# Levels 1 to 4 of a block inverse by 32x32 tiles, biases as a row of the low-rank products, and both square roots under one table

## The reference

```python
w_log = -jax.nn.softplus(-(w0 + jnp.tanh(xw @ w1) @ w2).astype(f32)) - 0.5
decay = jnp.exp(-jnp.exp(w_log))
a = jax.nn.sigmoid((a0 + (xa @ a1) @ a2).astype(f32))
kk = (k * k_k).reshape(B_, S, H, N)
kk = kk / jnp.maximum(jnp.sqrt(jnp.sum(kk * kk, axis=-1, keepdims=True)), L2_EPS)
k = k * (1.0 + (a - 1.0) * k_a)
def step(state, inp):
    sa = jnp.einsum('bhvk,bhk->bhv', state, -kk_t)
    state = (state * w_t[:, :, None, :] + sa[..., None] * (kk_t * a_t)[:, :, None, :]
             + v_t[..., None] * k_t[:, :, None, :])
    return state, jnp.einsum('bhvk,bhk->bhv', state, r_t)
mean = jnp.mean(o, axis=-1, keepdims=True)
var = jnp.mean(jnp.square(o - mean), axis=-1, keepdims=True)
o = ((o - mean) * lax.rsqrt(var + GN_EPS)).reshape(B_, S, D) * gn_w + gn_b
```

## Time and profile before

| | |
|---|---|
| runs | 2527.18, 2533.05, 2538.43 us, median 2533.05 |
| profiled execution | 2530.33 us, its span 2528.5 us |
| TensorE products busy | 2459.0 us, 97% of the span |
| VectorE, ScalarE, POOL busy | 1500.5 us (59%), 1252.0 us (50%), 185.5 us (7%) |
| mean granted TensorE clock | 0.994 |
| pipeline of the groups | from about 2180 to 2418 us of the span |

### The profile page before, as it was taken

The page is one execution under the profiler, slowest core; times in us unless marked ns, Lnnn a source line. Parts: engine busy times, 40 slices in busy tenths (PEclk is TensorE's granted clock), DMA queues, the critical chain, the costliest instruction groups (busy, mean ns, idle before and its releaser), DMA issues.

```text
span 2528.5 us, 39190 instructions
## 1 busy us (share of the span) xinstructions
PE 2459.0 (97%) x16044; PEld 2047.7 (81%) x16044; DVE 1500.5 (59%) x1985; ACT 1252.0 (50%) x1663; POOL 185.5 (7%) x218
## 2 busy tenths in 40 slices
PE   8999999999999999999999999999999999998898
PEld 7886888888888888887888888878788888887776
DVE  5457554584656666666444545445767555687766
ACT  5446444474555555555444444544445445565442
POOL 3002000000000000000000100000000001133330
PEclk9999999999999999999999999999999999999999
DMA  8756666555655555556555665544466677323352
GB/s 266 242 167 135 211 201 205 197 190 185 213 169 199 190 182 179 179 199 232 190 194 197 196 199 174 172 137 167 165 235 214 218 235 246 106 59 74 109 186 101
DMA packets 238570, 462.43 MB, mean 183 GB/s; under 512 B 10064, under 2 KB 32281, under 8 KB 236768
## 3 DMA queue, kind: packets, MB, share of 16 engines
q1 hardware_dynamic: 219280, 421.62, 50.5%
q0 software_dynamic: 18576, 38.28, 5.4%
q10 hardware_dynamic: 576, 0.53, 0.1%
HBM read 445.66 MB, written 14.74 MB: 182 GB/s over the span
## 4 chain that ended last, share of the span: by engine, by line
PE 44%; DVE 5%; ACT 3%; issue 1%; DMA 1%; SPq 0%; DVEq 0%; ACTq 0%
PE bank L418 12%; PE bank L419 12%; PE bank L420 12%; PE bank L2411 2%; DMA raw<-in_od_w_g 1%; DVE d_products L2368 1%; PE bank L2837 1%; ACT w_high L268 1%; PE bank L463 0%; PE bank L465 0%; PE bank L464 0%; DVE w_low L274 0%; SPq L2148 0%; PE bank L2239 0%; DVE d_steps L2430 0%
## 5 line engine op out<-in xcount | busy, mean ns | idle before, releaser
L274 DVE TENSOR_TENSOR w_low<-raw,w_high 128x1024 fp32r<-128x1024 f32 x768 | 928.7, 1222 | 784.7 <-ACT w_high L268 784.1
L268 ACT ACTIVATE w_high<-raw 128x1024 fp32r<-128x1024 f32 x768 | 804.5, 1057 | 911.6 <-PE bank L420 887.6
L418 PE MATMUL bank<-w_high,b_h_high 128*128 128x512 f32 x696 | 272.9, 392 | 0.0
L420 PE MATMUL bank<-w_high,b_h_low 128*128 128x512 f32 x696 | 271.1, 390 | 0.0
L419 PE MATMUL bank<-w_low,b_h_high 128*128 128x512 f32 x696 | 270.8, 389 | 0.0
L418 PE MATMUL bank<-w_high,a_h_high 128*128 128x512 f32 (+1 forms) x632 | 243.8, 386 | 0.0
L420 PE MATMUL bank<-w_high,a_h_low 128*128 128x512 f32 (+1 forms) x632 | 242.8, 384 | 0.0
L419 PE MATMUL bank<-w_low,a_h_high 128*128 128x512 f32 (+1 forms) x632 | 242.7, 384 | 0.0
L418 PE MATMUL bank<-w_high,c_x_high 128*128 128x512 f32 x496 | 195.3, 394 | 0.0
L420 PE MATMUL bank<-w_high,c_x_low 128*128 128x512 f32 x496 | 193.2, 390 | 0.0
L419 PE MATMUL bank<-w_low,c_x_high 128*128 128x512 f32 x496 | 193.0, 389 | 0.0
(11 more groups left out here) (463 smaller groups left out, 3765.9 us busy)
## 6 DMA issues: line engine op xcount, KB each, us to landing
raw<-in_w_up SPq DMA_DIRECT2D x88, 1024.0 KB, 5.1
raw<-in_w_in SPq DMA_DIRECT2D x75, 1024.0 KB, 5.2
raw<-in_ev_w_in SPq DMA_DIRECT2D x48, 1024.0 KB, 5.1
raw<-in_w_down SPq DMA_DIRECT2D x44, 1024.0 KB, 5.0
raw<-in_w_out SPq DMA_DIRECT2D x16, 1024.0 KB, 5.0
raw<-in_ev_w_out SPq DMA_DIRECT2D x16, 1024.0 KB, 5.0
raw<-in_od_w_r SPq DMA_DIRECT2D x16, 1024.0 KB, 5.9
raw<-in_od_w_k SPq DMA_DIRECT2D x16, 1024.0 KB, 5.0
```

The lines of the kernel that those rows point to most:

```text
L268: act.activation(wh[n % 4][:, :, 0:width], raw_half, ACT.Copy).then_inc(sem("w_high_made"), 1)
L274: vec.tensor_tensor(wl[n % 4][:, :, 0:width], raw_half, wh[n % 4][:, :, 0:width].bitcast(F32), ALU.subtract).then_inc(sem("w_low_made"), 1)
L418: pe.matmul(b, xh, wh[n][:, k % 2, 0:width], start=(c == 0 and k == 0), stop=False)
L420: mm = pe.matmul(b, xl, wh[n][:, k % 2, 0:width], start=False, stop=(c == j.chunks - 1 and k == 3))
```

## The change

Six things, all in segment D:

1. **Levels 1 to 4** work on the 32x32 blocks on the diagonal. A tile is 128x128 instead of 128x256; a stage has 32 products of 32x32 on the four diagonal tiles of the array in place of 16 of 64x64. VectorE's copies and transposes and ScalarE's copies of these levels are 128x128.
2. **Level 5** joins the two 32x32 blocks of a head: 5Y is one 32x32 product a block, 5T the old 64x64 one. VectorE makes its wide operand (`d_turned_wide`) by two masked copies of 128x256 ahead of the copies of 5Y.
3. **Bias.** w0 and a0 are a 97th row of the low-rank weights, against a row of ones that POOL writes once; the sigmoids read the banks. The additions L2311 and two loads of 128 rows go, two of one row come; the wait of SP for stage 1T goes.
4. **Roots together.** The square and its sum for group n+2 move into halves 9 and 10 of round n, the root behind them, ahead of the sigmoid table of half 1; the square-root table is loaded behind the exponential of prep part 5, and the post-norm's root loads none.
5. **Mean.** The division by 64 and the subtraction are one instruction.
6. The steps' tile is filled in six pieces, and the mask tables are laid out anew.

```diff
@@ TensorE, level_pe
-            for h in range(4):
-                for b in range(2):
-                    s = slice(64 * b, 64 * b + 64)
-                    if stage == "Y":
-                        left, right = MB[n % 2][t][s, h, 0:64], XI[n % 2][t][s, h, :]
-                    else:
-                        left, right = YI[k - 1][t][s, h, :], x[s, h, :]
-                    op = pe.matmul(PS[t][s, 64 * h:64 * h + 64], left, right, start=True, stop=True)
+            if k < 5:
+                op = block_products(pe, n, k, stage, t)
+            else:
+                for h in range(4):
+                    for b in range(2):
+                        if stage == "Y":
+                            upper, lower = slice(64 * b, 64 * b + 32), slice(64 * b + 32, 64 * b + 64)
+                            op = pe.matmul(PS[t][lower, 32 * h:32 * h + 32], MB[n % 2][t][upper, h, 32:64],
+                                           XI_BLOCKS[n % 2][t][upper, h, :], start=True, stop=True)
+                        else:
+                            s = slice(64 * b, 64 * b + 64)
+                            op = pe.matmul(PS[t][s, 64 * h:64 * h + 64], LAST_I[s, t, h, :], WIDE[s, t, h, :],
+                                           start=True, stop=True)
+    def block_products(pe, n, k, stage, t):
+        for h in range(4):
+            for i in range(4):
+                s, own = slice(32 * i, 32 * i + 32), slice(32 * (i % 2), 32 * (i % 2) + 32)
+                if stage == "Y":
+                    left = MB[n % 2][t][s, h, own]
+                    right = XI[n % 2][t][s, h, own] if k == 1 else XI_BLOCKS[n % 2][t][s, h, :]
+                else:
+                    left = YI[k - 1][t][s, h, :]
+                    right = T0[t][s, h, own] if k == 1 else T_BLOCKS[0][t][s, h, :]
+                op = pe.matmul(PS[t][s, 32 * h:32 * h + 32], left, right, start=True, stop=True)
@@ VectorE, level_vec, ahead of the copies of 5Y
+            for t in range(2):
+                inc(vec.copy_predicated(WIDE[:, t, :, :].rearrange("p h (c s) -> p h c s", c=2),
...
@@ ScalarE, prep_act
         if part == 2:
-            await_step(act, "prep_vec", "lora_a", n)
-            act.activation(tw[:, :, :], tw[:, :, :], ACT.Sigmoid)
-            inc(act.activation(ta[:, :, :], ta[:, :, :], ACT.Sigmoid))
+            await_step(act, "prep_pe", "lora", n)
+            for i, dst in enumerate((tw, ta)):
+                op = act.activation(dst[:, :, :], PS[6 + i][:, :].rearrange("p (t n) -> p t n", t=2), ACT.Sigmoid)
+            inc(op)
...
         if part == 5:
             await_step(act, "prep_vec", "cs_before", n)
             inc(act.activation(tq[:, :, :], tq[:, :, :], ACT.Exp, scale=-C))
+            if n >= 1:
+                act.preload_act_table_set("sqrt_and_others")
@@ the order
-    ACT_AHEAD, ACT_BEHIND = {1: [1], 2: [2]}, {3: [3, 4], 4: [5], 6: [6], 7: [7]}
-    VEC_AHEAD, VEC_BEHIND = {3: [3]}, {1: [1], 2: [2], 4: [4], 5: [5], 10: [8]}
+    ACT_AHEAD, ACT_BEHIND = {1: [8], 2: [2]}, {3: [4], 4: [5], 6: [6], 7: [7]}
+    VEC_AHEAD, VEC_BEHIND = {3: [3]}, {1: [1], 4: [4], 5: [5], 10: [8]}
     POOL_AHEAD, POOL_BEHIND = {}, {4: [4], 5: [5]}
+    PE_NEXT, ACT_NEXT, VEC_NEXT, POOL_NEXT = {10: [1]}, {9: [1], 10: [3]}, {10: [2]}, {8: [1]}
@@ VectorE, post_vec
-            inc(vec.tensor_scalar(m, m, 1.0 / 64, None, ALU.mult))
-            await_step(vec, "post_vec", "mean", n)
-            inc(vec.tensor_tensor(by_head(OO), by_head(OO), wide(m), ALU.subtract))
+            inc(vec.scalar_tensor_tensor(out=by_head(OO), in0=wide(m), scalar=-1.0 / 64, in1=by_head(OO), op0=ALU.mult,
+                                         op1=ALU.add))
```

More of the change, by code:

```diff
@@ L84, in constant_tables @@
     q, m = r[:, None] % 64, r[None, :64]
[L85 to L88, removed]
+    t["level0"] = ((m == q + 1) & (q % 2 == 0)).astype(np.float32)
+    for k in range(1, 5):
+        a, b = (r[:, None] % 32) >> k, r[None, :32] >> k
+        t[f"level{k}"] = ((a == b + 1) & (b % 2 == 0)).astype(np.float32)
+    t["level5"] = np.tile((q >= 32).astype(np.float32), (1, 32))
+    t["ident_rows"] = (r[:, None] % 32 == r[None, :32]).astype(np.float32)
+    t["own_blocks"] = (q // 32 == m // 32).astype(np.float32)
     t["ident_blocks"] = (q == m).astype(np.float32)
@@ L2117, in build @@
         "post_act": ["squares", "root"],
-        "post_vec": ["sum", "mean", "centre", "var", "eps", "inverse", "norm"],
+        "post_vec": ["sum", "centre", "var", "eps", "inverse", "norm"],
         "post_pool": ["bonus", "gain", "bias", "with_bonus", "out"],
@@ L2638, in build, with pipeline @@
     PE_AHEAD, PE_BEHIND = {3: [2]}, {6: [6], 7: [7]}
-    ACT_AHEAD, ACT_BEHIND = {1: [1], 2: [2]}, {3: [3, 4], 4: [5], 6: [6], 7: [7]}
-    VEC_AHEAD, VEC_BEHIND = {3: [3]}, {1: [1], 2: [2], 4: [4], 5: [5], 10: [8]}
+    ACT_AHEAD, ACT_BEHIND = {1: [8], 2: [2]}, {3: [4], 4: [5], 6: [6], 7: [7]}
+    VEC_AHEAD, VEC_BEHIND = {3: [3]}, {1: [1], 4: [4], 5: [5], 10: [8]}
     POOL_AHEAD, POOL_BEHIND = {}, {4: [4], 5: [5]}
-    def pipeline(eng, level, state, prep, post, score, first, last, ahead, behind, begin):
+    PE_NEXT, ACT_NEXT, VEC_NEXT, POOL_NEXT = {10: [1]}, {9: [1], 10: [3]}, {10: [2]}, {8: [1]}
+    def pipeline(eng, level, state, prep, post, score, first, last, ahead, behind, following, begin):
         for n in range(GROUPS + 1):
@@ L2667, in pipeline @@
                     first(eng, n + 1, SCORE_AT[half])
-                if prep is prep_pe and (half == 10 and n + 2 < GROUPS):
-                    prep(eng, n + 2, 1)
+                if n + 2 < GROUPS:
+                    for part in following.get(half, ()):
+                        prep(eng, n + 2, part)
                 if n < GROUPS and half == R0_AT:
@@ L2988, in prep @@
                 prep_act(act, n, 4)
+            if n == 1 and part == 8:
+                part = 1
+            if n == 1 and part == 2:
+                prep_act(act, n, 3)
+                prep_act(act, n, 8)
             prep_act(act, n, part)
@@ L2997, in last @@
                 split_units(act, True, jo, half - 6, 1)
[L2998 removed]
+        pipeline(act, level_act, state_act, prep, post_act, idle, idle, last, ACT_AHEAD, ACT_BEHIND, ACT_NEXT,
+                 begin)
         split_units(act, True, jo, 3, 1)
@@ L3100, in d_vec, with prep @@
             first_turned(vec, 0, t)
+        def prep(vec, n, part):
+            if n == 1 and part == 1:
+                prep_vec(vec, n, 2)
+            prep_vec(vec, n, part)
         def begin(vec, half):
```

130 lines of the change are left out of this document (76 added, 54 removed).

## The result

The changed kernel takes **2555.13 us** (median of 5 runs, 2546.24 to 2555.79) against 2532.22 (5 runs, 2527.18 to 2538.43): ratio 1.0089, 95% interval 1.0077 to 1.0101. It is 0.9% slower; I had forecast 2521 and a range up to 2534. The profiled execution took 2555.13 us, its span is 24.8 us longer than before's (2553.3 against 2528.5).

The account below looks back on a forecast made before the run. The recurrence was taken as the place to gain, VectorE carrying most; 11.4 us from six rounds, plus 0.5 and 1.7 at the ends, minus 1.5 for fetching, made 12.1: 2521 us against the 2533.05 median, range 2506 to 2534.

Parts of the forecast that it names:

- Fetching: Term for more or longer issue gaps on TensorE from added instructions: 0.2 us a round, 1.5 us in all.
- Rival 5: Clock: shorter stages idle TensorE more; a fifth of each round at half speed costs about 1 us; 2528 us; 5%.
- stretch A: Round's first copy to the state's scalings, 8.18 us in round 1; forecast 1.3 us shorter, with TensorE the later chain.
- The stage: TensorE's 32x32 stage of 64 records in levels 1 to 4: 0.60 us, bounds 0.48 and 0.97.
- Rival 1: Products become the bound: records keep 30.6 ns, a level stage takes 1.96 us; 2568 us, slower; 5%.
- rival 2: Issuing limits the level stage: 0.97 us for twice as many instructions; 2527 us; 12%.
- Round 0: First round: the root's table now precedes ScalarE's filling of level 3's tile; additions go; 0.5 us charged.
- The table load: Sign: ScalarE loads the square-root table right before the copy of o0, 1.28 us.
- no wait at the reciprocals: Sign: VectorE no longer waits at the reciprocals in a round; no size was given.
- The wait for the level 3 transposes: Sign: VectorE waits 0.5 to 1 us ahead of level 3's transposes.
- B's price of nothing: Scalings to o's addition, 6.63 us: narrower tiles' 0.8 us saving is spent waiting for the square-root table; gain 0.
- Rival 3: Fetching takes the gain: one more issue gap each round costs 1 to 1.5 us; 2530 us, at worst slower; 13%.

Follow-up runs that it names:

- no tiles: The change without its 32x32 tiles, keeping bias row, roots together and merged mean over the old 64x64 levels: 2527.1 us, ratio 0.9981 to before.
- half the products: The change leaving out the products of two of four heads in levels 1 to 4, copies and transposes kept: 2522.0 us, ratio 0.9954 to before.
- three heads: The change leaving out the fourth head's products in levels 1 to 4, copies and transposes kept: 2537.9 us, ratio 1.0020 to before.
- padded: The kernel before plus 16 small unused products in each stage of levels 1 to 4, without 32x32 tiles: 2573.9 us, ratio 1.0169.
- ordered kernel: The change without 32x32 tiles, with round 0's step-table fills ahead of ScalarE's root and sigmoid table loads: 2523.2 us, ratio 0.9965 to before.
- late table: The ordered kernel with the square-root table loaded behind the first two copies of turned rows, not ahead of o0's: 2524.8 us, ratio 0.9977 to before.
- wide products: An unused 128x128 by 128-column product ahead of the first tile's products, each stage, levels 1 to 4: ordered kernel 2535.9 us, the change 2553.3.

## Why the prediction was wrong, point by point

**The sum failed at "Fetching".** It charged 0.2 us a round for the added instructions. Measured are 4.32 - 1.42 = 2.9 us a round, and 21.4 us from 2060 to 2440. I had the facts in the earlier trace rows: waits up to 2.5 us, and 43 packets. What I did not do was to set the time in which TensorE uses a packet up against the time that the next one takes to come. q8 in the same 240 us of the changed kernel:

```profile
q8 instruction: 54, 0.88, 1.5%
```

The packet records show that the packets are what TensorE waits for. Count its instructions in order (products, weight loads, its own waits for semaphores) in blocks of 256, the content of a packet. All 21 "issue" waits of the changed kernel then stand, within one instruction, at the seam of two blocks, and each ends 1.2 to 1.6 us after a packet of q8 has landed. The same holds for the 9 waits of the kernel before (1.2 to 1.6 us) and for those of every other kernel here, with 32x32 tiles or without (1.0 to 1.6 us).

In the changed kernel a packet on time starts 1.1 us (median) after TensorE has taken up the block before it, and takes about 1 us. Some start more than 2 us after it; I call these late. Packets that start from 2180 to 2440 us:

| kernel | time for 256 instructions of TensorE, "issue" waits left out, us | late packets, of all | "issue" waits, us |
|---|---|---|---|
| before | 5.7 | 10 of 45 | 11.8 |
| no tiles | 5.7 | 10 of 45 | 7.3 |
| half the products | 5.6 | 12 of 45 | 18.9 |
| three heads | 4.9 | 12 of 53 | 19.1 |
| padded | 4.4 | 11 of 55 | 19.8 |
| the change | 3.9 | 12 of 58 | 33.3 |

The late packets are nearly as many before (10) as in the change (12), and start as late (3.6 and 3.2 us in the mean). **What the change altered is how long a block lasts, 3.9 us for 5.7:** a packet that is late is now missed for longer, 26.6 of the 33.3 us stand at late packets, and some that are on time are missed too. In the longest case TensorE took up a block at 2250.98 us, the next packet started at 2255.86 and landed at 2256.83:

```profile
2258.25 0.32 PE L2445 MATMUL bank<-d_turned_blocks,d_steps 32*32 32x32 f32 x4 [5.28 <-issue]
```

In the 1.2 us before a late packet starts, the 16 DMA engines are 92% (before) and 74% (the change) busy with other transfers; before the other packets it is 11% and 7%. That the loads hold the packets up is my reading of this coincidence; no run moved the loads or changed the supply. The table also shows what it does not explain: half the products waits 18.9 us with blocks as long as those of the kernel without tiles (7.3 us). Its late packets start 3.6 us behind instead of 3.0 and are two more, in one execution of each.

The pace alone would have been a warning. No two packets start less than 3.3 us apart in this trace, 26 ns for a record with its weight load. The mean of a round (942 records in 32.5 us, 35 ns each) is slower than that, so averages hide it; from 1T on, 176 records took 3.32 us (2211.14 to 2214.46, where 2Y stopped), 19 ns each.

**Not in the sum at all: the clock.** Rival 5 priced half speed at some 8 us a round and a fifth of each round in it at 1 us. The fifth came: a clock of 0.89 is 22% of the six rounds at the lower level, against 4% before. The price was too low. TensorE's stages got shorter by 0.98 - 0.69 = 0.29 us, eight a round, 2.3 us less work; its busy time stayed the same, so about 2.4 us a round of busy time went into the lower clock, 0.89 against 0.98; not all of it need lie on the path. In stretch A of round 1 waits and clock came together, and "1.3 us less" became 4.3 more.

**The stage: 0.60 forecast, 0.69 measured.** The column-bound end was right, 7.2 ns a record against 7.6; the fixed part was 0.23 us, not 0.1. The same lengths come back in every round at full clock. Rival 1 (30.6 ns a record) and rival 2 (0.97 us a stage) are refuted. The Trainium skill ("TensorE: Matmul & The Clock Gate", Back-to-back issue gap) gives about 25 ns from start to start for short products; this trace disagrees, with 7.2 ns a record on four tiles. The 2550 us that rival 1 worked out from that figure is 2545 by its own rule (eight stages 0.62 us longer, 26.3 + 5.0 - 29.7 = 1.5 us a round, eight rounds).

**Round 0: 0.5 us forecast.** By its trace the ordered kernel takes 2.8 us less there, by the ratios (0.9981 to 0.9965) 4 us, with intervals that overlap. I had counted one table ahead of level 3's fill; there were two ahead of level 2's fill as well.

**What was right.** The table load stands right ahead of L2630's copy of o0, there are three table loads a round, and VectorE has no wait at the reciprocals. The wait for the level 3 transposes came too (1.19 us for 0.5 to 1), but by luck: in round 1 the table was loaded at 2228.34, ScalarE then idled 0.26 us for TensorE, and stage 3T itself began only at 2228.48. B's price of nothing fits the late table, which gained nothing. Without tiles, and ordered, a round is 29.76 - 28.27 = 1.5 us shorter, though half of that is less "issue" (0.70 for 1.42) in these two executions; bias, roots and mean, with round 0 in order, give 8.9 us of the 12 I had hoped for from everything. What would show the forecast wrong was also named: "issue" waits well above today's in sum.

**Rival 3 was the case,** with too small a price: one more gap of 1 to 1.5 us a round, 2530. It was twice that (2.9 us a round, 21 waits for 9), and the clock fell beside it.

## What to carry to other kernels

Before work is cut into more and smaller products, divide TensorE's instructions in the trace into blocks of one packet (256 here) and see how long a block will last in the new kernel. Compare that with the time from taking up a block to being able to use the next: here about 3.5 us for a packet on time (1.1 to its start, 1 to its landing, 1.2 to 1.6 more), and over 7 us in the worst case while loads run. A mean over the round does not show it. Here four times smaller products with twice as many instructions bought 2.3 us of array time a round, paid 2.9 in waits for instructions, and had some 2.4 us more of busy time at the lower clock. Try the parts of a change that take instructions away apart from the part that adds them: those alone, with round 0 in order, were worth 8.9 us.

## What the runs showed of the hardware

- Records of 32x32 products on four diagonal tiles follow at 7.2 ns each behind a fixed 0.23 us a stage (0.46, 0.55, 0.69 us for 32, 48, 64 records).
- Instructions come in packets of 16 KB, 64 bytes each, never closer than 3.3 us in the changed kernel's trace. Every "issue" wait of TensorE stands at the seam of two blocks of 256 of its instructions and ends 1.0 to 1.6 us after a packet has landed; the longest took 5.3 us, in the middle of a stage.
- Packets that start late (over 2 us after TensorE took up the block before) do so where the DMA engines are busy with other transfers, 92% and 74% against 11% and 7% before the other packets.
- With 687 records a round, half as wide in the levels, the granted clock was 0.89, with 685 of the old width 0.98; TensorE's idle time differed too (5.5 and 2.8 us a round), so the cause is not told apart.
- The changed kernel, where the clock is down and instructions are late, took in wide products that cost 13 us elsewhere without getting longer (ratio 1.0086 against 1.0089).
